# Hybrid HGRN2 and block-sparse attention decoder step: VectorE's order in the fused key stage, transposes of the key units first, lower weight part second

## The reference

```python
h = rmsnorm(x, g_pre1) * (1.0 + sc1) + sh1
proj = jnp.dot(h, w_in)
hq, hf, hi, hg, aq, ak, av, ua, ub = jnp.split(proj, splits, axis=-1)
o_a, s_new = hgrn2_recurrence(...)                  # gated linear recurrence, 4 heads of 128
k_past = cache_k[l][page_table]...                  # 8 sequences x 2048 positions x 8 heads x 64
gate = einsum('bhqd,bnhd->bhqn', qh, kmean)         # block means pick 3 blocks of 256
s_sel = einsum('bhqd,bhqkld->bhqkl', qh, k_sel)     # scores against cached keys
o_b = softmax over chosen and own blocks, times v
merged = sigmoid(ua) * dot(o_a, w_proj_a) + sigmoid(ub) * dot(o_b, w_proj_b)
x = x + gt1 * rmsnorm(dot(merged, w_out), g_post1)
x = x + gt2 * rmsnorm(dot(silu(g) * u, w_down), g_post2)      # g, u from w_gu
```

## Time and profile before

| | |
|---|---|
| median of 3 runs | 751.43 us (750.09 to 752.02) |
| the profiled execution | 755.44 us, span 753.6 us |
| TensorE busy | 641.5 us, 85% of the span |
| VectorE busy | 414.8 us, 55% |
| ScalarE busy | 274.6 us, 36% |
| GpSimd busy | 74.8 us, 10% |
| moved by DMA | 168.98 MB, mean 224 GB/s |
| transposes of keys (L994) | 64, 75.0 us, 1217 ns each |
| lower weight part (L865) | 128, 156.0 us, 1237 ns each |

### The profile page before, as it was taken

The page is one execution under the profiler, slowest core; times in us unless marked ns, Lnnn a source line. Parts: engine busy times, 40 slices in busy tenths (PEclk is TensorE's granted clock), DMA queues, the critical chain, the costliest instruction groups (busy, mean ns, idle before and its releaser), DMA issues.

```text
span 753.6 us, 13191 instructions
## 1 busy us (share of the span) xinstructions
PE 641.5 (85%) x5260; PEld 539.9 (72%) x5260; DVE 414.8 (55%) x529; ACT 274.6 (36%) x388; POOL 74.8 (10%) x82
## 2 busy tenths in 40 slices
PE   4678998678888878968987599955999999999995
PEld 1275997657777767933332299935999999999993
DVE  0751577676666875755862247476453535341526
ACT  1432434342233433525132223343454545332412
POOL 2140010042333600000000000003000000000000
PEclk9979999999899998989699689987999999999998
DMA  9969834878677786689999977700555555747501
GB/s 334 413 253 349 305 105 134 272 247 275 224 239 260 256 266 217 219 278 346 311 306 341 364 265 227 255 1 4 166 166 167 167 167 167 278 138 254 168 1 63
DMA packets 98007, 168.98 MB, mean 224 GB/s; under 512 B 7121, under 2 KB 38537, under 8 KB 95778
## 3 DMA queue, kind: packets, MB, share of 16 engines
q1 hardware_dynamic: 92082, 162.86, 64.1%
q10 hardware_dynamic: 5152, 3.08, 1.3%
q0 software_dynamic: 720, 2.32, 0.8%
HBM read 163.51 MB, written 4.72 MB: 223 GB/s over the span
## 4 chain that ended last, share of the span: by engine, by line
PE 59%; DVE 19%; DMA 7%; issue 5%; SPq 5%; ACT 4%; POOL 1%; ACTq 0%; DVEq 0%
PE ps L1310 15%; PE ps L1312 15%; PE ps L1311 15%; DVE KT L994 6%; DMA ring<-w_in 4%; SPq L361 3%; ACT w_hi L553 2%; PE ps L1465 2%; DMA ring<-cache_v 2%; DVE w_lo L865 2%; PE ps L1328 1%; DMA ring<-w_ada 1%; SPq L327 1%; PE ps L1486 1%; PE ps L1472 1%
## 5 line engine op out<-in xcount | busy, mean ns | idle before, releaser
L865 DVE TENSOR_TENSOR w_lo<-ring,w_hi 128x1024 fp32r<-128x1024 f32 (+1 forms) x128 | 156.0, 1237 | 154.9 <-ACT w_hi L553 154.3
L1310 PE MATMUL ps<-h_hi,w_hi 128*128 128x288 f32 x704 | 216.2, 307 | 21.9 <-DVE w_lo L865 12.0
L1311 PE MATMUL ps<-h_lo,w_hi 128*128 128x288 f32 x704 | 211.4, 300 | 0.0
L1312 PE MATMUL ps<-h_hi,w_lo 128*128 128x288 f32 x704 | 210.6, 299 | 0.0
L553 ACT ACTIVATE w_hi<-ring 128x1024 fp32r<-128x1024 f32 (+1 forms) x128 | 131.5, 1042 | 161.6 <-PE ps L1312 71.6
L1310 PEld LDWEIGHTS ps<-h_hi,w_hi 128*128 128x128 f32 x704 | 136.1, 193 | 26.4 <-DVE w_lo L865 13.1
L1311 PEld LDWEIGHTS ps<-h_lo,w_hi 128*128 128x128 f32 x704 | 136.1, 193 | 0.6 <-issue 0.5
L1312 PEld LDWEIGHTS ps<-h_hi,w_lo 128*128 128x128 f32 x704 | 136.1, 193 | 0.0
L994 DVE STREAM_TRANSPOSE KT<-ring 128x1024 f32<-128x1024 f32 x64 | 75.0, 1217 | 0.9 <-DMA ring<-cache_k 0.8
L1465 PE MATMUL ps<-KT,Wk 128*32 128x128 f32 x1024 | 38.1, 294 | 34.5 <-DVE KT L994 34.0
L1465 PEld LDWEIGHTS ps<-KT,Wk 128*32 128x32 f32 x1024 | 28.7, 117 | 43.9 <-DVE KT L994 32.4
(11 more groups left out here) (294 smaller groups left out, 834.8 us busy)
## 6 DMA issues: line engine op xcount, KB each, us to landing
ring<-cache_k SPq DMA_DIRECT2D x128, 256.0 KB, 3.6
ring<-cache_v SPq DMA_DIRECT2D x128, 256.0 KB, 4.0
ring<-w_ada SPq DMA_DIRECT2D x24, 1024.0 KB, 10.2
ring<-w_in SPq DMA_DIRECT2D x44, 512.0 KB, 5.8
ring<-w_gu SPq DMA_DIRECT2D x44, 512.0 KB, 4.8
ring<-w_down SPq DMA_DIRECT2D x20, 512.0 KB, 4.5
ring<-w_out SPq DMA_DIRECT2D x8, 512.0 KB, 5.9
S<-state_hgrn SPq DMA_DIRECT2D x4, 512.0 KB, 6.1
```

The source lines that it names most:

```text
L865: dve.tensor_tensor(w_lo[:, s, k, :], slot4(s)[:, k, :], w_hi[:, par, k, :].bitcast(F32), ALU.subtract).then_inc(sem("lo_split"), 1)
L1310: pe.matmul(dst, h, x_hi, start=first, stop=False)
L1311: pe.matmul(dst, h, x_lo, start=False, stop=False)
L1312: return pe.matmul(dst, l, x_hi, start=False, stop=last)
```

## The change

In each of the 22 steps VectorE first runs `turn_keys(u)` for all units of the step, then `lo_wh(w + 1, half)`, then the `block_sums`, which for a step with two units stood between or behind the transposes. The other engines' programs are the same.

```diff
@@ -1032,9 +1032,10 @@
             link(dve.memset(hAs[:, :, :], 0.0))
             for w in FUSED:
                 for half in range(2):
+                    for u in units(w, half):
+                        turn_keys(u)
                     lo_wh(w + 1, half)
                     for u in units(w, half):
-                        turn_keys(u)
                         if u % 4 == 0 and u >= 8:
                             block_sums(u // 4 - 2)
                     if (w, half) == (8, 1):
```

## The result

| | before | changed |
|---|---|---|
| median | 751.72 us (4 runs, 750.09 to 753.11) | 715.69 us (4 runs, 714.90 to 719.89) |
| profiled execution | 755.44 us, span 753.6 | 714.90 us, span 713.1 |
| ratio of the times | | 0.9533, 95% interval 0.9491 to 0.9575 |

The account below looks back on a forecast made before the run. TensorE was taken to be held up by VectorE's key transposes, queued behind w_lo. Waits -34.0, residue +8 and clock -4 gave -30.0 us, from a median of 751.43 to 721.4 us, range 712.5 to 733.5.

Parts of the forecast that it names:

- The waits for KT are removable: Fused key stage: all 34.0 us that TensorE waits for transposes before the key scores can go.
- w_lo costs nothing behind the transposes: VectorE's order: w_lo, later by 2.4 or 4.7 us, has the whole next step as slack and costs nothing.
- The residue of 8 us in the first third: Key stage: waits that stay, 6.4 us up to step (11, 0) plus 1.6 later; ends 3 and 18.
- The walk: Start of the key stage: remaining waits worked out for units 1, 4, 6, 7, 9 and 10, 6.4 us in all.
- The clock, minus 4 us: TensorE in the key stage: fewer gaps win back 4 of 9.4 us lost at 1.2 GHz; ends 0 and 9.4.
- The sum: Whole kernel: -34.0 + 8 - 4 = -30.0 us, making the median 721.4 us; chance 0.67.
- The sum that the prediction gave by this rule: Whole kernel: the skill's clock rule taken alone returns all 9.4 us, so the gain would be 35.4 instead of 30.
- This loop is cut: Loop transposes, SP, w_in, w_hi, w_lo, transposes: reordering breaks it, so ScalarE's 27.3 us of w_in waits cost nothing.
- Transfers: Rival: DMA transfers pace the key stage at 270 GB/s, gain 22.7 us, 728.7 us; chance 0.17.
- One sign of being wrong: Key stage: the forecast is wrong if transposes wait for cache_k by over 10 us.
- The slower case: Rival: transposes at VectorE's head wait for pages, holding w_lo; stage 14.7 us longer, 766.1 us; chance 0.04.
- VectorE as the pace: Rival: VectorE's fixed order paces the key stage, gain only 12 us, 739.4 us; chance 0.09.

Follow-up runs that it names:

- e1: Changed kernel with the block sums left between and behind the units as before, so only w_lo is moved: 715.35 us, ratio 0.9472.
- e2: Kernel before, with the new VectorE order only in steps from w = 13 on (12 of 22 steps): 733.55 us, ratio 0.9707.
- e4: Changed kernel, but SP issues key loads of unit u + 2 only after w_lo of the step that turns unit u: 772.97 us, ratio 1.0250.
- e9: Changed kernel with each step's w_in load ahead of its key loads on SP: 747.21 us, ratio 0.9889.
- e5: Changed kernel with w_lo moved to the end of each step, behind block sums, keep and one-time work: 717.71 us, ratio 0.9505.
- e6b: Kernel before, with 112 filler matmuls in five of TensorE's longest waits for KT, changing no output: 751.22 us, ratio 0.9966.
- e3: Kernel before, with ScalarE copying w_hi ahead of the previous step's score rows; VectorE's order unchanged: 745.79 us, ratio 0.9872.
- e8: Kernel before, with w_hi copied ahead of the score rows and, on SP, each w_in load ahead of the step's key loads: 746.65 us, ratio 0.9926.
- a1: The changed kernel itself, run again on another occasion as a comparison: 718.66 us, ratio 0.9517 against the kernel before.
- b2: Changed kernel with sums back between units and transposes of units 0 and 1 some 10 us earlier, ahead of the stage: 710.33 us, ratio 0.9420.
- e7: Changed kernel with 11 first halves of units turned twice, about 13.8 us more VectorE work: 728.12 us, ratio 0.9650.

## Why the prediction was right, and where it was off

- **The waits for KT are removable.** Right. 34.0 us were named, 28.2 went; e1 and e2 show that they go with w_lo's place, and in the steps where it is moved. e4 and e9 show the condition: the key loads must leave with the transposes.
- **w_lo costs nothing behind the transposes.** Right: TensorE waits 0.4 us for it, and 0.2 in e5, where it goes last.
- **The residue of 8 us in the first third.** 5.8 us, in units 1, 2, 3, 4, 6 and 7. The walk had the places of units 1, 4, 6 and 7; units 2 and 3, in time by its working, waited 0.8 and 0.3 for their last pages, and 9 and 10 didn't wait. It gave `keep` a step of slack and put its delay at nothing; `keep` had none, and TensorE's waits for `hA` rose from 2.4 to 4.2 us.
- **The clock, minus 4 us.** This is the term that was mis-sized. TensorE's busy time in the stage fell by 12.3 us, three times the 4 and more than the whole 9.4 that the granted clock of 0.94 gave for it. Two steps of its working failed. It took the 12% at 1.2 GHz as 12% of the busy time, 18.8 us; but the lower level lay on 23.9 us of the stage, and TensorE was busy in 22.5 of them, so half of that, 11.3 us by my estimate, was lost. And it held back more than half for gaps outside the keys, while in the changed kernel the stage's clock is 1.00. The last 1.0 of the 12.3 us stays open; outside the stage, where nothing was changed, the busy time fell by 3.0 us as well (482.1 to 479.0). e6b shows the effect by itself, smaller: 5.6 us of the work's busy time, 2.5 us of the medians.
- **The sum.** With 28.2 - 1.8 + 12.3 = 38.7 it is what the stage shows. In the terms of the profiled executions 30.0 us were forecast and 40.5 came (8.3 more from the clock, 2.2 from the residue, 1.7 outside the stage, 1.8 less for `hA`); that the medians miss by 6.0 only is in part chance, the two profiled executions lying 4.5 us further apart than the medians. The Trainium skill (TensorE: Matmul & The Clock Gate, section Part 1: The HAM clock gate) says that activity lifts the half rate. The trace agrees: with 26.5 us of idle time gone, no half rate is left in the stage. The sum that the prediction gave by this rule, 35.4 us, came nearest to the 36.0 of the medians.
- **"This loop is cut".** Right in its effect, too simple as a picture. e3 takes away one condition of w_hi and gains 1.3%: the loop through SP and w_in stays closed, at 53.0 us of waits. e8 takes w_in out of it and gains 0.7%, but holds the key loads behind each projection, so whether w_in alone closes the loop stays open. e4 and e9 show the part that was priced at nothing: the earlier key loads are no by-product but a condition of the gain.
- **The rivals.** Transfers: the stage now moves 293 GB/s at a share of 0.87, above the 270 at which that rival set its ceiling; this ceiling did not hold. It was read from few stretches: before the change, 252 to 262 us already moved 304 GB/s. One sign of being wrong did show: transposes wait for cache_k by 10.2 us (11.8 in a1), over the 10 that the prediction allowed. The gain came all the same, so the sign was set too tight; but key pages are now 6% of the chain, and b2, which sends two units' loads earlier, is faster. The slower case did not come, but its mechanism is real, as e4 made it happen with 65.1 us of waits for pages. VectorE as the pace, 0.09 with 12.0 us against 14.2 a pair of steps, was rejected on an average. It didn't hold back the gain, yet e7 shows that VectorE has little to spare at the head of a step. Whether its order or the arrival of key pages bounds next, the runs don't separate. With the clock back, TensorE needs 147.16 / 11 = 13.4 us a pair, not 14.2, against 135.51 / 11 = 12.3 for VectorE.

## What to carry to other kernels

When an engine serves two consumers in a fixed order, put first what is wanted in this step, and second what has a step of slack, above all if the second waits for a third engine. Check what the served piece releases: here an early transpose frees a ring half, and holding that load back turned a gain of 36 us into a loss of 18. Before you move a load in a queue, look at what it waits for there: everything behind it waits too, as in e8. Price gaps of TensorE at more than their length if the granted clock of the stretch is below 1: here 26.5 us of idle time went, and 12.3 us of busy time with it.

## What the runs showed of the hardware

The clock: the 1024 small matmuls on `KT` kept TensorE busy for 38.1 us before and 33.5 after, with means of 294 and 275 ns for one, which overlap; for the 112 of L1525 the means are 301 and 280 ns. Fillers of 13.4 us in 37.0 us of gaps gave back 5.6 of the 12.3 us in the profiles, with the doubt stated at e6b.

VectorE and GpSimd: the w_lo at 180.92 took 2.15 us where its median is 1.19, while GpSimd's two products beside it took 3.51. GpSimd in the changed kernel, 176 to 192 us:

```profile
180.70 3.51 POOL L487 TENSOR_TENSOR hx<-hx,proj 128x512 f32<-128x512 f32 x2
```

From 112 to 300 us the mean of its 14 products of L487, this shape and one other, rose from 1396 to 1783 ns. Both instructions read two operands from SBUF. The Trainium skill (SBUF — State Buffer, section Who interferes with whom) states that a VectorE instruction with two SBUF inputs and a GpSimd instruction that reads SBUF exclude each other; these rows agree. It did reach TensorE here: by my estimate the `keep` behind that w_lo began 1 us later for it (2.15 less 1.19), and TensorE waited 0.81 us for `hA` at 184.34.
